# Up projection of a gated MLP with seven half products in place of eight, on one Trainium2 core

## What is computed

```python
def conv_gated_mlp(h, w_up, conv_w, w_down):          # h 1024 x 1024, w_up 1024 x 5632, w_down 2816 x 1024
    u = causal_dwconv(h @ w_up, conv_w)               # three taps along the tokens, for each column
    gt, val = jnp.split(u, 2, axis=-1)                # 2816 columns each
    return (jax.nn.silu(gt) * val) @ w_down
```

## Time and profile before

| quantity | value |
|---|---|
| time, three runs | median 1189.08 us (1187.56 to 1189.5) |
| profiled execution: its own time; its span | 1189.45 us; 1187.4 us |
| PE / PEld busy share of the span | 96% / 80% |
| DVE / ACT / POOL busy share | 59% / 48% / 31% |
| up projection on PE | about 711 to 1019 us, the beginning of three units before it |
| down projection on PE | about 1019 to 1181 us |
| mean granted TensorE clock | 0.99 |

### The profile page before, as it was taken

How to read it: one execution, slowest core, us unless ns; L and a number is a source line. 1 busy time by engine, 2 the same in 40 slices (tenths; PEclk the granted TensorE clock), 3 DMA queues, 4 the chain that set the end, 5 groups by cost and what they waited for, 6 DMA issues and landing times.

```text
span 1187.4 us, 22866 instructions
## 1 busy us (share of the span) xinstructions
PE 1142.1 (96%) x9511; PEld 944.9 (80%) x9530; DVE 703.3 (59%) x982; ACT 566.7 (48%) x1055; POOL 369.6 (31%) x379
## 2 busy tenths in 40 slices
PE   5999999899999999999998999999999999999997
PEld 5888879788887877878766878888888888888886
DVE  5788976656668785767546744333333333655755
ACT  7444332447565555465565644333333333544543
POOL 2477346213022121120232025444444555300000
PEclk9999999999999999999998999999999999999999
DMA  8245110500000000000114452222222222564661
GB/s 254 72 124 167 79 45 18 128 24 23 2 22 22 2 22 22 2 2 2 38 45 169 142 177 71 74 78 78 72 71 72 71 71 71 169 221 142 207 219 71
DMA packets 104078, 99.86 MB, mean 84 GB/s; under 512 B 15412, under 2 KB 89384, under 8 KB 103976
## 3 DMA queue, kind: packets, MB, share of 16 engines
q1 hardware_dynamic: 102536, 93.15, 25.7%
q10 hardware_dynamic: 1440, 5.24, 1.1%
HBM read 85.24 MB, written 13.11 MB: 83 GB/s over the span
## 4 chain that ended last, share of the span: by engine, by line
PE 87%; DVE 7%; ACT 3%; DMA 1%; issue 1%; POOL 0%; DVEq 0%; ACTq 0%
PE psum L1700 26%; PE psum L2008 13%; PE psum L2547 9%; PE psum L1347 8%; PE psum L1594 5%; PE psum L1527 4%; PE psum L2587 4%; PE psum L1543 4%; PE psum L1508 3%; DVE arena L2434 2%; PE psum L1340 1%; PE psum L1292 1%; PE psum L1274 1%; PE psum L1428 1%; PE psum L1410 1%
## 5 line engine op out<-in xcount | busy, mean ns | idle before, releaser
L1700 PE MATMUL psum<-h_p,up_p 128*128 128x512 f32 x704 | 221.0, 390 | 1.2 <-DVE arena L1676 0.7
L1700 PE MATMUL psum<-h_q,up_q 128*128 128x512 f32 x704 | 220.7, 389 | 0.0
L1817 DVE SCALAR_TENSOR_TENSOR arena<-psum,arena 128x1023 f32<-128x1023 f32 x44 | 56.5, 1283 | 196.1 <-ACT arena L1786 196.1
L1766 POOL TENSOR_TENSOR up_q<-arena,up_p 128x1024 fp32r<-128x1024 f32 x44 | 105.9, 2408 | 212.6 <-ACT up_p L1762 212.6
L1700 PEld LDWEIGHTS psum<-h_p,up_p 128*128 128x128 f32 x704 | 132.2, 188 | 29.4 <-POOL up_q L1766 1.1
L1700 PEld LDWEIGHTS psum<-h_q,up_q 128*128 128x128 f32 x704 | 132.1, 188 | 27.3
L1786 ACT ACTIVATE arena<-psum,arena 128x1024 f32<-128x1024 f32 x44 | 49.1, 1117 | 198.9 <-PE psum L1700 198.9
L1347 PE MATMUL psum<-arena 64*64 64x64 f32 x3072 | 110.8, 221 | 2.7 <-DVE arena L1123 1.5
L1347 PEld LDWEIGHTS psum<-arena 64*64 64x64 f32 x3072 | 97.5, 134 | 17.9 <-issue 6.8
L2008 PE MATMUL psum<-dn_p,ap_p 128*128 128x512 f32 x352 | 110.0, 392 | 0.4 <-DVE ap_q L1876 0.4
L2008 PE MATMUL psum<-dn_q,ap_q 128*128 128x512 f32 x352 | 109.7, 391 | 0.0
(11 more groups left out here) (304 smaller groups left out, 2154.0 us busy)
## 6 DMA issues: line engine op xcount, KB each, us to landing
arena<-in_ffn_w_up SPq DMA_DIRECT2D x44, 512.0 KB, 3.9
arena<-in_ffn_w_down SPq DMA_DIRECT2D x44, 512.0 KB, 3.7
arena<-in_w_in SPq DMA_DIRECT2D x20, 512.0 KB, 3.9
arena<-in_x SPq DMA_DIRECT2D x16, 512.0 KB, 5.5
qkv_mid<-arena ACTq DMA_DIRECT2D x9, 512.0 KB
arena<-qkv_mid SPq DMA_DIRECT2D x8, 576.0 KB, 4.4
arena<-in_w_out SPq DMA_DIRECT2D x8, 512.0 KB, 3.7
x_mid<-arena SPq DMA_DIRECT2D x8, 512.0 KB, 3.4
```

Of the source, the lines that this page charges most:

```text
L1700: ins = pe.matmul(up_ps[j % 2][:, g, h * 512:(h + 1) * 512], w[:, k], x[:, k, h * 512:(h + 1) * 512], start=k == 0 and x is h2_p, stop=Tru ...
L1766: pool.tensor_tensor(up_q[up_slot(u)], up_st[up_slot(u)], up_p[up_slot(u)], ALU.subtract).then_inc(late("up_lo")[0], 1)
L1817: v.scalar_tensor_tensor(out=y[:, 1:S], in0=ps[:, 0:S - 1], scalar=tap(1, u), in1=y[:, 1:S], op0=ALU.mult, op1=ALU.add).then_inc(late("up_ ...
```

## The change

The weights of a pair and the activations are each seen as two by two: gate or value block and inner half (4 blocks k each) for the weights, inner half and token half for the activations. The plain way is eight half products of 4 blocks, p and q, 512 tokens. For pairs 5 to 21 (17 of them, `SEVEN`) the Strassen-Winograd form with seven is used: products 1 to 7, each 8 matmuls of 512 tokens. Pairs 0 to 2 keep the old code; pairs 3 and 4 have four pieces a1, a2, b1, b2 of 16 matmuls, through the new ring of slabs.

- Activation sums (`whole`, `t_sum`, ACT `t_hi`, `t_lo`): four of them, each 128x2048, are formed and split once, during pairs 0 to 4.
- Weight sums (`weight_sum`, step s): four per pair, 128x512, on DVE, both inputs in SBUF.
- Splits (steps h on ACT, l on POOL) go by product: seven of 128x512 a pair, into a ring of five slabs. A slab is free when the product five before it is done.
- Products 1, 6, 7, 4 accumulate one upon another in one PSUM bank; 2 in a second; 5 and 3 in a third. What has to be added elsewhere is copied out by ACT (step k, after 1, 6 and 7) and added by DVE back into PSUM (step a, for 2, 5 and 3; the sum for 5 goes to a fourth bank).
- Taps and Silu stay as they were (t and y on ACT, c and v on DVE). The product of the halves (step p) moves from POOL to DVE for pairs from 3 on. It is written to one of two buffers `y_b`, and SP stores it to DRAM (step x) for pairs 3 to 20; the down projection reads it back by token half, 256 KB each (`act_reload`), two kk ahead of the weight load it stands behind.
- Each engine takes its steps from one list, `UP_ORDER`. PE's order in a pair is 5, 6, 2, 7, product 1 of the next pair, 4, 3. A step is a letter, the product or g, and the pair: h2.13 is the ACT split for product 2 of pair 13.
- In the down projection the first two kk are taken over tiles 0 and 1, then 2, then 3, and the slots of `dn_st` and `ap` lie elsewhere.

```diff
+CLASSIC = 3
+RING = 5
+UP_KINDS = "ccsssssssssssssssss"
+SEVEN = [j for j in range(CLASSIC, NF) if UP_KINDS[j - CLASSIC] == "s"]
+A1, A2, B1, B2 = "a1", "a2", "b1", "b2"
...
+def up_order():
+
+    order = []
+    for j in range(CLASSIC, NF):
+        if j in SEVEN:
+            own = [(i, j) for i in (1, 5, 6, 2, 7, 4, 3)]
+        else:
+            own = [(i, j) for i in (A1, A2, B1, B2)]
+        if j - 1 in SEVEN:
+            order.insert(len(order) - 2, own.pop(0))
+        order += own
+    return order
...
+    "l5.12 a5.11 y10 s6.12 h2.12 s7.12 k1.12 l2.12 h6.12 p10 h7.12 l6.12 t1.11 a3.11 x10 h1.13 l7.12 c1.11 t0.11 l1.13 s3.12 h4.12 "
+    "c0.11 k6.12 l4.12 h3.12 v1.11 l3.12 d14 a2.12 s5.13 k7.12 v0.11 h5.13 l5.13 a5.12 y11 s6.13 h2.13 s7.13 k1.13 l2.13 h6.13 p11 "
+    "h7.13 l6.13 t1.12 a3.12 x11 h1.14 l7.13 c1.12 t0.12 l1.14 s3.13 h4.13 c0.12 k6.13 l4.13 h3.13 v1.12 l3.13 d15 a2.13 s5.14 k7.13 "
...
+    "h3.21 i0 l3.21 e1 a2.21 f0 v0.20 i1 g0 k7.21 v1.20 y20 a5.21 i2 p20 f1 t1.21 g1 j0 x20 f2 a3.21 c1.21 t0.21 g2 j1 c0.21 v1.21 "
+    "v0.21 y21 p21 "
...
+        slab_at = (23552, 24576, 25600, 31744, 32768)
+        slab_p = [rounded(f"slab_p{n}", w, [HT, P]) for n, w in enumerate(slab_at)]
+        slab_q = [rounded(f"slab_q{n}", w + 512, [HT, P]) for n, w in enumerate(slab_at)]
+        u_s = {1: R.view(33792, [HALF]), 7: R.view(34304, [HALF]), 6: R.view(23040, [HALF])}
+        y_a = R.view(19456, [S])
+        y_b = [R.view(w, [S]) for w in (27648, 26624)]
...
+        def spill(sp, j):
+            prod_done(sp, j)
+            sp.dma_start(act_mid[j], y_b[j % 2]).then_inc(late(f"act_st{j % 2}")[0], 16)
...
+        def split_mult_hi(act, i, j):
+            n = mult_at(i, j)
+            if n >= RING:
+                act.wait_ge(*late("up_mm", 2 * CLASSIC + n - RING + 1))
+                act.wait_ge(*late("up_mm", 2 * CLASSIC - 1))
+            if i in (3, 5, 6, 7):
+                sum_done(act, i, j)
+            else:
+                pair_landed(act, j)
+            act.activation(slab_p[n % RING], part_source(i, j), ACT.Copy, scale=1.0 - SPLIT_W).then_inc(late("up_hi")[0], 1)
...
+        def split_mult_lo(pool, i, j):
+            n = mult_at(i, j)
+            pool.wait_ge(*late("up_hi", 3 + HIGHS.index(("h", i, j)) + 1))
+            pool.tensor_tensor(slab_q[n % RING], part_source(i, j), slab_p[n % RING], ALU.subtract).then_inc(late("up_lo")[0], 1)
...
+            def tap_(g, j):
+                if j < CLASSIC:
+                    act.wait_ge(*late("up_mm", 2 * j + g + 1))
+                elif j in SEVEN:
+                    for i in ((2, 3), (5,))[g]:
+                        add_done(act, i, j)
+                    mult_done(act, (3, 4)[g], j)
                 else:
-                    dn_split_hi(act, u + 3 - NU)
-                if u == NU - 3:
-                    act_split_hi(act, 0)
-                    act_split_hi(act, 1)
-                if u == NU - 1:
-                    act_split_hi(act, 2)
...
+            def copied(i, j):
+
+                mult_done(act, i, j)
+                before = max((x for x in SEVEN if x < j), default=None)
+                if before is not None:
+                    add_done(act, {1: 2, 6: 3, 7: 5}[i], before)
+                act.activation(u_s[i], mult_ps(i, j), ACT.Copy).then_inc(late("c_cp")[0], 1)
...
+            T_FROM = {5: (0, 0), 7: (0, 1), 6: (1, 1), 4: (1, 0)}
+
+            def whole(i):
+                if i in (6, 4):
+                    v.wait_ge(*late("up_mm", 2))
+                v.scalar_tensor_tensor(out=t_f[i], in0=x_quad(h2_p, *T_FROM[i]), scalar=1.0 / SPLIT_W - 1.0, in1=x_quad(h2_q, *T_FROM[i]),
...
+            def t_sum(i):
+                x, y = {5: (7, 5), 7: (6, 7), 6: (6, 5), 4: (4, 6)}[i]
+                for z in (x, y):
+                    t_made(v, "W", z)
+                if i != 5:
+                    t_made(v, "S", {7: 5, 6: 7, 4: 6}[i])
+                v.tensor_tensor(t_f[i], t_f[x], t_f[y], ALU.subtract).then_inc(late("t_f")[0], 1)
+
+            def t_lo(i):
+                v.wait_ge(*late("t_hi", T_HIS.index((i,)) + 1))
+                v.scalar_tensor_tensor(out=t_q[i], in0=t_p[i], scalar=1.0 - 1.0 / SPLIT_W, in1=t_f[i], op0=ALU.mult, op1=ALU.add)                    .then_inc(late("t_lo")[0], 1)
...
+            def weight_sum(i, j):
+                if i == 5:
+                    pair_landed(v, j)
+                    if seven_before(j) is not None:
+                        part_done(v, 3, seven_before(j))
+                    out, x, y, op = s_e1[j % 2], w_of(j, 1, 0), w_of(j, 1, 1), ALU.add
+                elif i == 6:
+                    sum_done(v, 5, j)
+                    out, x, y, op = s_e2[j % 2], s_e1[j % 2], w_of(j, 0, 0), ALU.subtract
+                elif i == 7:
+                    sum_done(v, 5, j)
+                    out, x, y, op = w_of(j, 1, 0), w_of(j, 0, 0), w_of(j, 1, 0), ALU.subtract
                 else:
+                    sum_done(v, 6, j)
+                    part_done(v, 5, j)
+                    out, x, y, op = s_e1[j % 2], w_of(j, 0, 1), s_e2[j % 2], ALU.subtract
+                v.tensor_tensor(out, x, y, op).then_inc(late("s_add")[0], 1)
+
+            def added(i, j):
+
+                mult_done(v, i, j)
+                copy_done(v, {2: 1, 5: 7, 3: 6}[i], j)
+                out = c_ps(1, j)[:, right] if i == 5 else mult_ps(i, j)
+                v.tensor_tensor(out, mult_ps(i, j), u_s[{2: 1, 5: 7, 3: 6}[i]], ALU.add).then_inc(late("c_add")[0], 1)
...
+            def prod(j):
+                if j < CLASSIC:
+                v.wait_ge(*late("up_silu", SILUS.index((j,)) + 1))
+                conv_done(v, 1, j)
+                v.tensor_tensor(y_b[j % 2], y_a, y_b[j % 2], ALU.mult).then_inc(late("up_prod")[0], 1)
...
+            for n, (i, j) in enumerate(MULTS):
+                part_done(pe, i, j)
+                if i in (1, B1):
+                    conv_done(pe, 1, j - 2)
+                if i in (2, 5, A1):
+                    conv_done(pe, 0, j - 2)
+                if j < CLASSIC + 2 and i in (1, 2, 5, A1, B1):
+                    conv_done(pe, 1, j - 2)
+                if i in t_p:
+                    t_ready(pe, i)
+                if i in (6, 7):
+                    copy_done(pe, {6: 1, 7: 6}[i], j)
+                if i == 4:
+                    copy_done(pe, 7, j)
+                if i == 3:
+                    add_done(pe, 5, j)
+                for k in range(HT):
+                    if j in SEVEN:
+                        for w, x in ((slab_p[n % RING], x_p[i]), (slab_q[n % RING], x_q[i])):
+                            ins = pe.matmul(mult_ps(i, j), w[:, k], x[:, k], start=k == 0 and x is x_p[i] and i in (1, 2, 5),
+                                            stop=True, skip_group_check=True)
+                    else:
+                        g, kh = divmod((A1, A2, B1, B2).index(i), 2)
+                        for w, h in ((slab_p[n % RING], h2_p), (slab_q[n % RING], h2_q)):
+                            for th, part in enumerate((left, right)):
+                                ins = pe.matmul(c_ps(g, j)[:, part], w[:, k], x_quad(h, kh, th)[:, k],
+                                                start=k == 0 and h is h2_p and kh == 0, stop=True, skip_group_check=True)
+                ins.then_inc(late("up_mm")[0], 1)
...
+        def act_reload(sp, kk):
+            m, k = divmod(kk, NF)
+            n = RELOADS.index(kk)
+            if n >= 4:
+                act_landed(sp, RELOADS[n - 4])
+            sp.dma_start(act_rows(kk), act_mid[k][:, HT * P * m:HT * P * (m + 1)]).then_inc(sem(f"act_ld{n % 4}"), 16)
...
         def down_loads(sp):
-            for kk in range(3):
-                sp.wait_ge(*late("up_lo", NU - 2 + kk))
-                down_load(sp, kk)
-            for s in range(2):
-                sp.wait_ge(sem(f"x1_st{s}"), 16 * NT // 2)
-            sp.wait_ge(*late("up_mm", NU))
+            mult_done(sp, 4, SEVEN[-1])
+            down_load(sp, 3)
+            for j in range(CLASSIC, NF - 1):
+                spilled(sp, j)
+            sp.wait_ge(*late("up_mm", 2 * CLASSIC + PRODUCTS))
+            add_done(sp, 3, SEVEN[-1])
+            for kk in RELOADS[:3]:
+                act_reload(sp, kk)
...
-            for kk in range(3, DN):
-                if kk >= 4:
-                    dn_ready(sp, kk - 4)
+            for kk in range(4, DN):
+                dn_ready(sp, kk - 4)
                 down_load(sp, kk)
+                if kk + 2 in RELOADS:
+                    act_reload(sp, kk + 2)
...
+                late_tiles = tiles[2:] if m or NF - 1 in SEVEN else tiles[:1:-1]
+                for part in (tiles[:2], late_tiles[:1], late_tiles[1:]):
                     for k in range(2):
                         ready(k0 + k)
                         for t in part:
                             if k == 0 and m:
                                 pe.wait_ge(*late("f_y", t - HT + 1))
```

(82 more changed lines are left out.)

197 lines of the change are left out of this document (154 added, 43 removed), and 24 rows, old and new, of the table UP_ORDER.

## The result

The changed kernel takes **1168.87 us** (median of 4 runs, 1166.44 to 1169.5) beside 1189.15 us for the kernel before in the same series (1187.56 to 1189.5): a ratio of 0.9828, with a 95% interval of 0.9811 to 0.9845. A second series of five rounds gave 1167.63 and 0.9821 [0.9808, 0.9834]. The profiled execution took 1169.29 us, its span was 1167.5 us (1187.4 before). The forecast was 1167.5.

The account below looks back on a forecast made before the run. PE was taken as the bound, through its count of matmuls: 1189.45 - 30.8 + 5.1 (pairs) + 1.5 (start) + 2.5 (turn) = 1167.8, median 0.4 lower, so 1167.5 us. Own range 1161 to 1174, overall range 1159 to 1187.

Parts of the forecast that it names:

- The removal: Up projection: 17 pairs need 56 matmuls in place of 64, saving 136 at 0.2267 us, 30.8 us.
- Nothing for met waits and for eight matmuls into one bank: PE in the pairs by seven: no surcharge for either; met waits bounded at some 0.1 us a product, 12 us.
- The pauses in the pairs: Pairs by seven: 1.3 us of stall in one pair in four, 0.3 a pair, 5.1 us for 17 pairs.
- the turns of DVE and POOL: Pairs by seven: DVE instructions with two SBUF inputs and POOL's block each other, whole instructions at a time; mean wait 0.44 us.
- its walk through a pair: One pair by seven followed step by step: DVE without waits does a3, c1, s3, c0, v1 from 0.3 to 5.0 us.
- one pair in four at 1.3: Steps s6, s7, p on DVE wait 1.3 us too long if POOL always has work; taken for one pair in four.
- The turns are 98% full: Pairs by seven: POOL's splits and DVE's two-input SBUF instructions together need 12.5 of 12.69 us.
- My rival of 1180 us: Turns go against DVE at s6, s7, p, in all pairs or half: 1174 to 1187 us; chance 0.20.
- The start: Pairs 0 to 4: the slab of a2.3 waits for sum S6, ready 745 to 749, wanted at 747.3; 1.5 us.
- The turn: Change to the down projection: PE waits 0.9 for j1, 0.6 for v1, 0.6 at kk 2; taken as 2.5 us.
- My 0.6 for v1 and 0.6 for kk 2: Turn to the down projection: PE waits 0.6 us for tap v1 and 0.6 us at kk 2.
- The down projection: Unchanged in length but for the pauses at the turn; 36 reloads covered at no cost, DMA share 0.77.

Follow-up runs that it names:

- the run with eight products: Changed kernel with product 3 done twice in each of the 17 pairs, so 64 matmuls a pair again: 1193.29 us, 1.004 of the kernel before.
- the read that costs 5.1 us: Changed kernel plus one POOL subtraction of two 128x512 SBUF blocks, behind the split for product 6 in pairs 5 to 19: 1173.95 us.
- the fills that cost none: Changed kernel plus three POOL fills of 128x512, which read nothing, behind the split for product 6 in pairs 5 to 19: 1168.74 us.
- The exchanges: Changed kernel with product 6's splits ahead of product 2's, 1170.07 us; with v1 ahead of c0, 1167.79; both with W4 later and turn reordered, 1167.71.
- a few exchanged entries: Changed kernel with W4 later, product 6 first in pairs 9 to 14, v1 first in pairs 5 to 19, and the turn reordered: 1163.92 us.

## Why the prediction was right, and where its terms were off

**The removal** (30.8 us) held: the pitch is unchanged in the new form, and the run with eight products gives the 30.8 back but for the pauses that it makes room for. Nothing for met waits and for eight matmuls into one bank was a choice with a bound of 12 us. The 56.00 us for 248 matmuls bear it out, and the 0.5 us of small pieces over 119 products, 0.004 us each, is all that is left for it.

**The pauses in the pairs** were put at 5.1 and measured 4.3 us. The reason, the turns of DVE and POOL, is shown by the read that costs 5.1 us and the fills that cost none, but for the 1.0 us ahead of product 4 in the last pair, which stays with eight products too. The places were partly right: ahead of product 6 for POOL (0.30 and 0.38 us in pairs 9 and 13). Those of product 1 for v1 (0.32 to 0.64 in pairs 16 to 19) the prediction named among the releasers, but its walk through a pair has v1 done early. Not in it at all were the 0.94 in the last pair, where product 4 waits for the copy of product 7 because no product 1 of a next pair lies between, and the 0.33 ahead of product 5 there. It was not one pair in four at 1.3 either, but eight waits of mostly 0.3. That so many small waits add up to nearly the 5.1 of a few large ones is partly luck.

**"The turns are 98% full" was too high.** Groups by shape from 790 to 980 us of the kernel after:

```profile
L2000 POOL TENSOR_TENSOR slab_q<-arena,slab_p 128x512 fp32r<-128x512 f32 x104 | 163.2, 1601 | 30.3 <-ACT slab_p L1993 30.2
L2123 DVE TENSOR_TENSOR arena<-arena 128x512 f32<-128x512 f32 x58 | 62.8, 1098 | 0.0
L2130 DVE TENSOR_TENSOR psum<-psum,arena 128x512 f32<-128x512 f32 x45 | 31.0, 689 | 7.9 <-PE psum L2176 5.2 <-ACT arena L2057 2.6
L2140 DVE TENSOR_TENSOR arena<-arena 128x1024 f32<-128x1024 f32 x14 | 26.0, 1854 | 0.0
L2057 ACT ACTIVATE arena<-psum 128x512 f32<-128x512 f32 x44 | 26.0, 592 | 32.9 <-PE psum L2176 32.9
```

The mean wait of a sum is 1.10 - 0.68 = 0.42 us, as worked out (0.44), and the PSUM additions and copies cost what the earlier trace rows gave. But a split on POOL that met one DVE sum took 1.75 us and not 1.27 + 0.61, and one that met the product 2.28 and not 1.27 + 1.13. Measured against one that met nothing, 1.29, a meeting costs 0.46 and 0.99 us, some 0.15 less than I charged. So the turns fill, by this estimate, about 7 x 1.29 + 4 x 0.46 + 0.99 = 11.9 of 12.69 us, and POOL did wait for ACT 30.3 us in this stretch of 15 pairs, 2 us a pair. The room is 0.8 us by this budget, and 1.0 to 1.7 by the extra read. My rival of 1180 us rested on the 98% and was thereby too likely.

How turns look in a pair (DVE and then POOL over time, kernel after):

```profile
901.71 2.64 DVE L2123 TENSOR_TENSOR arena<-arena 128x512 f32<-128x512 f32 x2
904.28 2.32 DVE L2140 TENSOR_TENSOR arena<-arena 128x1024 f32<-128x1024 f32 x1
906.52 0.69 DVE L2130 TENSOR_TENSOR psum<-psum,arena 128x512 f32<-128x512 f32 x1
...
910.68 1.26 DVE L2084 SCALAR_TENSOR_TENSOR arena<-psum,arena 128x1022 f32<-128x1022 f32 x1
...
912.47 0.68 DVE L2123 TENSOR_TENSOR arena<-arena 128x512 f32<-128x512 f32 x1
```

```profile
900.80 11.18 POOL L2000 TENSOR_TENSOR slab_q<-arena,slab_p 128x512 fp32r<-128x512 f32 x7 [1.98 <-ACT slab_p L1993]
```

Two sums take 2.64 in place of 1.3, the product 2.32 in place of 1.21; the addition with one side in PSUM keeps its 0.69 while POOL runs. When POOL is done, at 912, a sum takes 0.68 again. Seven splits take 11.18, 2.3 over 7 x 1.27. The tap at 910.68 is the v1 that product 1 of pair 16 waits for, until 912.09: it is late because DVE stood in turns before it.

**The start** (1.5 put, 1.4 measured) happened as told, slab a2.3 behind W4's turn; PE went on at 749.05, the upper end of the 745 to 749.

**The turn** was put at 2.5 and measured 4.2: the term that was mis-sized. DVE over time:

```profile
993.52 0.68 DVE L2253 SCALAR_TENSOR_TENSOR ap_q<-ap_p,arena 128x512 fp32r<-128x512 f32 x1
...
997.11 2.24 DVE L2253 SCALAR_TENSOR_TENSOR ap_q<-ap_p,arena 128x512 fp32r<-128x512 f32 x1
```

POOL over the same time:

```profile
993.71 5.09 POOL L2214 TENSOR_TENSOR dn_q<-arena,dn_p 128x1024 fp32r<-128x1024 f32 x2 [1.36 <-ACT dn_p L2204]
```

PE waits 2.52 us for the second of DVE's, j1. I had given it 0.61 us; it took 2.24, since POOL was in the second down split of this row, from 996.45 to 998.80. I had counted the turns in the pairs and not here. The rest, 1.6 us, is the clock, below. My 0.6 for v1 and 0.6 for kk 2 didn't come.

**The down projection** came out as told: no wait, reloads free, at a DMA share of 0.70 for the 0.77 forecast.

So the three terms, put at 9.1 us, measured 9.9: a turn too cheap by 1.7 and pairs too dear by 0.8. In the spans it adds up: 1187.4 - 30.8 + 9.9, with 0.5 us of small pieces and the 0.5 us by which the stage begins later, is 1167.5, as measured. The sum of the forecast, 1167.8, lay 1.5 us under the profiled execution, and the forecast 1.4 under the median. What stays open: whether an order of all pairs exists that also takes out the 3.1 us that are left in them. The exchanges mostly moved the pauses, which is what one expects of a few steps that are late by tenths everywhere; it doesn't prove that no order is better.

## What to carry over

Where two engines read SBUF by turns, cost the turns as a budget of their own beside each engine's busy time, and take the price of a meeting from the length of the instruction that was met, less a handover of some 0.15 us here. Count the meetings at the transitions as well: there one long instruction of the other engine stands ahead of the one that PE waits for, and a few exchanged entries gave 3.7 us. Local exchanges in the steady part mostly moved the pauses from one product to another. Where a profile names the releaser of a wait for several semaphores, look up when each of the awaited steps ended. To see whether room is there at all, run an extra read and an extra fill, or one product more.
